# A hybrid decoder layer on one core: in-projection, shift and RWKV preparation as one program, the sample recurrence on VectorE, two places for the scores of short prompt rows

## The reference, cut to what matters

```python
h = rmsnorm(x); proj = h @ w_in                      # 1056 x 3328, 26 tiles of 128 rows
q, k, v, pr = split(proj)                            # 12 tiles attention, 14 tiles RWKV
m = pr + (shifted - pr) * mu                         # token shift: r, k, v, xw, xa, xg
w = exp(-exp(-softplus(-(w0 + tanh(xw) @ w2)) - .5)) # decay
a = sigmoid(a0 + xa @ a2); g = sigmoid(xg) @ g2
kk = k * k_k / norm(k * k_k);  k = k * (1 + (a - 1) * k_a)
# state, per head 64 x 64, over tokens:
s = s * w + (s @ -kk) (kk * a)^T + v k^T;  y = s @ r
bonus = sum(r * k * r_k) * v;  y = (groupnorm(y) + bonus) * g
# differential attention: softmax(q1 k1) - lam * softmax(q2 k2), causal for the prompt,
# over 1024 cached keys (8 pages) + 4 new ones for each sample group
x = x + rmsnorm(concat(attention, y) @ w_o)
# then a gated convolution FFN and a per-layer embedding, both with residuals
```

## Time and profile before

| what | value |
|---|---|
| median of 3 runs | 2543.29 us (2535.67 to 2544.15) |
| profiled execution, its own time | 2543.07 us |
| its span, first to last instruction | 2541.6 us |
| TensorE busy | 2033.1 us (80%) |
| VectorE busy | 1200.1 us (47%) |
| ScalarE busy | 855.9 us (34%) |
| GpSimd busy | 470.2 us (19%) |
| mean granted clock of TensorE | 0.874 |

### The profile page before, as it was taken

How to read it: one execution, slowest core, us unless ns; L and a number is a source line. 1 busy time by engine, 2 the same in 40 slices (tenths; PEclk the granted TensorE clock), 3 DMA queues, 4 the chain that set the end, 5 groups by cost and what they waited for, 6 DMA issues and landing times. The chain is left out here.

```text
span 2541.6 us, 39506 instructions
## 1 busy us (share of the span) xinstructions
PE 2033.1 (80%) x15324; PEld 1930.0 (76%) x15324; DVE 1200.1 (47%) x1772; ACT 855.9 (34%) x1422; POOL 470.2 (19%) x600
## 2 busy tenths in 40 slices
PE   1999963449999882546485669899999999999996
PEld 1999962338888881435254559899999999999996
DVE  5001016635555426996321135586543376653365
ACT  3111114313333322334201134554433355543342
POOL 0000002442313118990231200000000000000000
PEclk8999986769999955767766579999999999999998
DMA  2222222010000004103495024243234343233343
GB/s 99 92 84 101 84 102 99 37 32 1 0 0 0 0 16 98 37 13 84 156 332 160 35 79 147 75 150 129 89 103 131 110 157 121 92 97 117 94 131 123
DMA packets 83863, 229.34 MB, mean 90 GB/s; under 512 B 13394, under 2 KB 15186, under 8 KB 83442
## 3 DMA queue, kind: packets, MB, share of 16 engines
q1 hardware_dynamic: 72690, 191.25, 23.6%
q0 software_dynamic: 8864, 30.84, 3.3%
q10 hardware_dynamic: 2176, 5.42, 0.7%
HBM read 189.74 MB, written 37.73 MB: 89 GB/s over the span
## 5 line engine op out<-in xcount | busy, mean ns | idle before, releaser
L2403 PE MATMUL tl_acc<-tl_Hh,tl_wh 128*128 128x264 f32 x1536 | 438.9, 286 | 7.3 <-DVE tl_Hl L2681 7.3
L2403 PE MATMUL tl_acc<-tl_Hh,tl_wl 128*128 128x264 f32 x1536 | 437.1, 285 | 0.0
L2403 PE MATMUL tl_acc<-tl_Hl,tl_wh 128*128 128x264 f32 x1536 | 437.0, 284 | 0.0
L2723 DVE TENSOR_TENSOR tl_wl<-tl_raw,tl_wh 128x1024 fp32r<-128x1024 f32 (+2 forms) x184 | 208.3, 1132 | 422.9 <-ACT tl_wh L2552 422.7
L2552 ACT ACTIVATE tl_wh<-tl_raw 128x1024 fp32r<-128x1024 f32 (+2 forms) x184 | 181.0, 984 | 499.1 <-PE tl_acc L2403 450.9
L2403 PEld LDWEIGHTS tl_acc<-tl_Hh,tl_wh 128*128 128x128 f32 x1536 | 289.2, 188 | 8.5 <-DVE tl_Hl L2681 8.3
L2403 PEld LDWEIGHTS tl_acc<-tl_Hh,tl_wl 128*128 128x128 f32 x1536 | 290.0, 189 | 0.0
L2403 PEld LDWEIGHTS tl_acc<-tl_Hl,tl_wh 128*128 128x128 f32 x1536 | 289.4, 188 | 0.0
L690 PE MATMUL in_acc<-Hh,in_wh 128*128 128x352 f32 x624 | 202.6, 325 | 24.5 <-DVE in_wl L673 24.5
L690 PE MATMUL in_acc<-Hl,in_wh 128*128 128x352 f32 x624 | 201.1, 322 | 0.0
L690 PE MATMUL in_acc<-Hh,in_wl 128*128 128x352 f32 x624 | 201.0, 322 | 0.0
(11 more groups left out here) (359 smaller groups left out, 4446.9 us busy)
## 6 DMA issues: line engine op xcount, KB each, us to landing
tl_raw<-dram_w_up SPq DMA_DIRECT2D x88, 512.0 KB, 3.5
as_kT<-dram_k_pool SPq DMA_DIRECT2D x64, 256.0 KB, 5.0
as_vp<-dram_v_pool POOLq DMA_DIRECT2D x64, 256.0 KB, 4.9
tl_raw<-dram_w_down SPq DMA_DIRECT2D x32, 448.0 KB, 3.4
dram_projT<-in_out POOLq DMA_DIRECT2D x26, 528.0 KB, 3.0
in_raw<-dram_w_in SPq DMA_DIRECT2D x26, 512.0 KB, 3.5
ap_dup<-dram_projT SPq DMA_DIRECT2D x20, 512.0 KB, 8.1
tl_raw<-dram_w_pg SPq DMA_DIRECT2D x32, 320.0 KB, 3.2
```

What stands on the lines that cost most here:

```text
L2403: last = nc.tensor.matmul(out[:, n, 0:HP], w[:, u % 2, k, :], z, start=(begin and q == 0), stop=(end and q == 2))
L2723: tt(wl[:, u % 2, 0:kt], raw[:, u % 3, 0:kt], wh[:, u % 2, 0:kt].bitcast(F32), ALU.subtract).then_inc(S["residued"], 1)
```

## The change

Three parts.

**One program for stages 1 to 4.** A new function `front` takes the place of the constants' phases, `lam`, `rms_rows`, `scale_split`, `project` "in", `rwkv_mix`, `rwkv_prepare` and `SampleStates.dump`. The projection runs over half weight tiles (52 units `u`, 4 row blocks each), with three buffers for the raw weights. The columns are split into 512 (`accA`, two buffers) and two times 272 (`accB`, one buffer). `Hh`/`Hl` are made from x times gain without R, and VectorE multiplies by R when it evicts a tile (`evict`). The tiles come in another order: xw/xa and xg first, then v, k, r of each pair, then the 12 of attention. An evicted tile is mixed from SBUF without being read back. The preparation goes in 8 pieces (4 pairs, columns 0 to 511 and 512 to 1055), a piece in 5 steps, and each unit from 12 to 51 carries one step on each engine. NR, B and K, and V go to new HBM tensors (`nrS`, `bkS`, `vS`), and `rwkv_transitions` loads them: first the 128 columns of its first turn, then the rest.

**The sample recurrence** moves from GpSimd in `attend_prompt` to VectorE in `attend_sample`. It is cut into 16 parts, two a group; a sum over 64 is one `tensor_reduce` and no tree of additions. VectorE's loop over groups is written out in a new order.

**Scores.** In `attend_prompt` the units 1 and 3 of a head put their scores at column 512, and the units 1 to 3 wait for the exponential of two units before.

The diff, cut to its core (`rwkv_mix`, `rwkv_prepare` and `SampleStates.dump` are deleted as printed above; the preparation's steps on each engine hold the same operations as before over half the columns; `part_a` is 12 matmuls of 512 columns a unit, `part_b` 24 of 272; `PIECE_AT[q]` is 12 + 5q; `take` and `put` are a product and a sum over 128x2048, `read` a product and a `tensor_reduce`):

```diff
@@ attend_prompt @@
+        bank = lambda i: 512 if i in (1, 3) else 0
...
-        @block.gpsimd
-        def _(pool):
-            beside(pool, beside_done)
...
-                    if not early(j, u, 1):
+                    if not early(j, u, 1) and (i == 0 or i > 3):
                         pe.wait_ge(S["exped"], s * 2 - 1 + c)
+                    elif not early(j, u, 2):
+                        pe.wait_ge(S["exped"], s * 2 - 3 + c)
@@ attend_sample, VectorE @@
+            for n in range(NB):
+                fill(n, n % 2, n < 2)
+                beside(dve, 2 * n, S)
+                leave(n)
+                if n + 2 < NB:
+                    front(n + 2, n % 2, False)
+                beside(dve, 2 * n + 1, S)
@@ SampleStates @@
+    def decay(self, dve, t, S):
...
+        self.nc.vector.tensor_tensor(tmp[:], st[:], along_v(1), ALU.mult).then_inc(S["against_kk"], 1)
+        dve.wait_ge(S["against_kk"], t + 1)
+        self.nc.vector.tensor_reduce(sav[:], tmp[:], AX, ALU.add).then_inc(S["sa_summed"], 1)
+        self.nc.vector.tensor_tensor(st[:], st[:], along_v(0), ALU.mult).then_inc(S["decayed"], 1)
...
+    def recur(self, dve, part, S):
+
+        (self.decay, self.take, self.put, self.read)[part % 4](dve, part // 4, S)
@@ rwkv_transitions, SyncE and GpSimd @@
+            now, later = slice(0, 2 * C), slice(2 * C, SEQ)
+            for dst, src in ((BK, "bkS"), (V, "vS"), (NR, "nrS")):
+                sp.dma_start(dst[..., now], o[src][..., now]).then_inc(first_in, 16)
             for dst, src in consts:
                 sp.dma_start(dst[:], a[src]).then_inc(S["const_in"], 16)
+            for dst, src in ((BK, "bkS"), (V, "vS"), (NR, "nrS")):
+                sp.dma_start(dst[..., later], o[src][..., later]).then_inc(rest_in, 16)
...
+            pool.wait_ge(first_in, 48)
             place(0, 0, True)
...
+            pool.wait_ge(rest_in, 48)
             with pool.Fori(1, NCH // 2) as i:
@@ front, TensorE @@
+            def part_b(u, t, kh):
+                if kh == 0 and t:
+                    pe.wait_ge(S["evicted_b"], t)
...
+            for u in range(FU):
+                t, kh = u // 2, u % 2
+                if u == 2:
+                    spread_x()
+                for piece in piece_steps(u):
+                    prep(*piece)
+                pe.wait_ge(S["residued"], u + 1)
+                if kh == 0:
+                    part_a(u, t, kh)
+                    part_b(u, t, kh)
+                else:
+                    part_b(u, t, kh)
+                    part_a(u, t, kh)
+                if u == 1:
+                    totals()
@@ front, ScalarE @@
+            for u in range(FU + 1):
+                round_up(u + 1)
...
+                if u % 2 == 0 and 0 <= t < N_SHIFTED:
...
+                    nc.scalar.activation(dst_of(j), cur[:, t % 3], ACT.Copy, scale=omu[:, j:j + 1])\
...
+                for piece in piece_steps(u):
+                    prep(*piece)
@@ front, VectorE @@
+            for k in range(KD):
+                dve.wait_ge(S["high"], k + 1)
+                stt(Hl[:, k], X[:, k], param("g_mix_pre", KD)[:, k:k + 1], Hh[:, k].bitcast(F32), ALU.mult,
+                    ALU.subtract).then_inc(S["low"], 1)
...
+                    tt(acc[:], acc[:], sq[:, k % 2], ALU.add).then_inc(S["summed"], 1)
+            for u in range(FU + 1):
+                residue(u + 1)
...
+                t = u // 2 - 1
+                if u % 2 == 0 and 0 <= t < MT_IN:
+                    evict(t)
+                if u % 2 == 1 and 0 <= t < N_SHIFTED:
+                    mix(t)
...
+                for piece in piece_steps(u):
+                    prep(*piece)
```

More of the change, by code:

```diff
@@ L1154, in front, with fill @@
                                         ALU.mult).then_inc(S["combined"], 1)
-            def back(n, b, first):
+            def fill(n, b, first):
                 dve.wait_ge(S["turned"], n + 1)
@@ L1465, in rwkv_transitions @@
     S = {n: kit.sem("rt_" + n) for n in names}
+    first_in, rest_in = kit.sem("rt_first_in"), kit.sem("rt_rest_in")
     with ExitStack() as ctx:
@@ new lines, in read @@
+    def read(self, dve, t, S):
+        vec, st, tmp, ys = self.vec, self.st, self.tmp, self.ys
+        dve.wait_ge(S["added_v"], t + 1)
+        self.nc.vector.tensor_tensor(tmp[:], st[:], vec[:, t, 4, :].unsqueeze(1).broadcast_to([P, 32, 64]),
+                                     ALU.mult).then_inc(S["against_r"], 1)
+        dve.wait_ge(S["against_r"], t + 1)
+        self.nc.vector.tensor_reduce(ys[:, t, :], tmp[:], AX, ALU.add).then_inc(S["y_summed"], 1)
+    def recur(self, dve, part, S):
+        (self.decay, self.take, self.put, self.read)[part % 4](dve, part // 4, S)
+        if part == 4 * NT - 1:
+            dve.wait_ge(S["y_summed"], NT)
@@ L2829, in build @@
-        x_view = a["xT"].rearrange("(k p) t -> p k t", p=P)
-        proj = o["projT"].rearrange("(m p) t -> m p t", p=P)
-        with ExitStack() as ctx:
-            Hh = kit.sb(ctx, "Hh", [P, KD, T], F32R)
-            Hl = kit.sb(ctx, "Hl", [P, KD, T], F32R)
-            raw = weight_buffer(kit, ctx, "in", KD)
-            with ExitStack() as inner:
-                X = kit.sb(inner, "X", [P, KD, T])
-                R = kit.sb(inner, "R", [P, T])
-                rms_rows(kit, "rms_x", X, R[:], KD, ones[:], epsc[:, 0:1], ident[:],
-                         loads=[x_view[:, k] for k in range(KD)])
-                scale_split(kit, "split_x", X, KD, T, Hh, Hl, gain("g_mix_pre"), lambda k: R[:],
-                            ahead=first_units(raw, a["w_in"]))
-            parts = [(n * T3, T3) for n in range(3)]
-            project(kit, "in", MT_IN, KD, 1, a["w_in"], Hh, Hl, parts,
-                    lambda c: ToDram(kit, c, "in", parts, lambda m: proj[m] if isinstance(m, int) else
-                                     proj[ds(m, 1)].rearrange("a p t -> (a p) t")), raw)
+        ELC = kit.sb(top, "ELC", [P, NPAIR, NCH])
@@ L2850, in build @@
+        front(kit, a, o, par, param, ones[:], epsc, ident[:], identb[:], causal[:], blockcol[:], lam, ELC)
+        proj = o["projT"].rearrange("(m p) t -> m p t", p=P)
         kit.retire()
```

826 lines of the change are left out of this document (486 added, 340 removed).

## The result

| | before | changed |
|---|---|---|
| median | 2543.72 us (4 runs, 2535.67 to 2545.21) | **2346.97 us** (4 runs, 2343.28 to 2349.22) |
| ratio, with 95% interval | | **0.9231** (0.9208 to 0.9254): faster |
| profiled execution: own time, span | 2543.07, 2541.6 us | 2346.25, 2344.6 us |
| mean granted clock | 0.874 | 0.907 |

The prediction said 2354, with 2325 to 2425 as the range. SyncE's queue marks the borders of the stages. This is its timeline in the changed kernel (start, length, line, transfer): the first load of the transitions, the first of the sample attention, and the first transfer behind it. Between them stand the store of the prompt state, at 792.61, and the first load of the prompt attention, at 809.00.

A forecast was written before the change was run, and what follows sets the result against it. TensorE was taken to bound projection and tail, an engine-to-engine chain the preparation. Savings of 158.7 (front) and 72.2 (prompt), less 4 (transitions) and 37.6 (sample), make 189.3 off 2543.07: 2354 us, range 2325 to 2425.

The forecast's parts named there:

- likeliest case: Whole kernel: the forecast itself, 2354 us, given a chance of 76%.
- Front, start: Before TensorE's full stream: x arrives earlier, VectorE passes over 8 row blocks; full stream from 28.5 us, 32 us earlier.
- Front, stream: Projection on TensorE: 51 units 289.7 us, ramp 3, row sums and spreading 5.7, small products 45, waits 3.
- the cover: Front: read-back, mix and preparation work on VectorE, ScalarE and GpSimd lie under TensorE's stream, costed at nothing.
- the first rival: Front: the preparation does not stay hidden, TensorE waits out the chain; 71 us come back, 2425 us; chance 12%.
- Front, end: After the last product: eviction 0.8 us, turning 4.18, copy 3.35, then 4.38 to the next stage, reached at 387.6.
- the transitions: Transitions stage: new loads ahead of the constants delay the first placing; 4 us lost, 0 to 20.
- Prompt attention: Prompt attention without GpSimd's recurrence: earlier first peak, heads of 34 and 48.4 us; 72.2 us saved, 62 to 78.
- The scores' places: Prompt attention: the two places of the scores were costed at nothing, TensorE being held and ScalarE waiting for the load.
- Sample attention: Sample attention with the recurrence on VectorE: 119 us from the first fill, 84 before; 37.6 us lost, 32 to 44.
- TensorE's clock in the front: Front: waits at each unit could drop TensorE to its lower clock; all at 1.2 GHz gives 2694 us; chance 3%.
- V pages were not held up: Sample attention: VectorE's recurrence passes could delay GpSimd's page issues, some 55 us more, 2409 us; chance 8%.

## Why the prediction was right

Its total is 7 us above the measured time and its likeliest case is the one that came. By its own steps:

**Front, start** (28.5 predicted, 30.4 measured). The issue, arrival and rounding of x took longer (VectorE's first `Hl` stands at 10.8, not 7), the pairs of passes were shorter (2.40, not 2.6), and the second unit waited for the queued residue as described, for 5.6 us. Errors of 3.8 us for the first and -1.9 for all passes make the 1.9.

**Front, stream** (346.4 predicted from the first full unit to the last product, 348.6 measured). The bare tile was 11.58 and not 11.36, 5.6 us over the 51 units; the small products came to 42 by the stores, 45 predicted. The granted clock was 0.83 from 30 to 60 us and 1.00 from 60 to 372, so 30 x 0.17, some 5 us, went to the ramp where 3 had been taken. The waits that I put at 3 us (0 to 15) do not appear: behind the start of the second unit TensorE waits for another engine only twice, 1.0 us each, for the row factor and, when the stream is over, for the last eviction. That 5.6 and 2 too little and 3 and 3 too much nearly cancel is luck. The work under the stream was as counted, 165 us of VectorE where the prediction had 166. So the cover held, and taking it away cost 92 us, more than the 71 that the first rival had for it. That price was too low because it took off TensorE's 59.4 us at the clock of 0.70, where the same products cost 42 to 45 in the stream, and because the chain of half pieces is 137 us long and not 130.

**Front, end** (12.7 predicted, 11.9 measured) and **the transitions** (4 and 3.3): right in size and in the sum for the latter. The prediction adds the loads of the first columns and of the constants to 10 us, and the first placing came at 10.1; with the order turned round it came at 10.5. The rest of the columns came sooner than predicted (34.3 us, not 43), and TensorE did not wait for it.

**Prompt attention** (72.2 and 72.8): the first peak, the heads of 34 and 48 us and ScalarE's wait in them came as written. Taking GpSimd's work back cost the 72 us again, and moving the load took the wait out of the heads. So this term is right in its mechanism and not only in its sum.

**The scores' places** (nothing, and nothing): right, though half of the reason given for it fell.

**Sample attention** (37.6 lost predicted, 30.0 measured): the term that missed most. It was 7.6 us too high, and the smaller errors of the other terms, the front's 3.3 us among them, cancel. A pass takes 2.27 to 2.29 us (2.3), the groups 15.2 to 15.6 and 14.5 to 15.2 (15.7 and 14.8), and the raw sum of 113.7 was 112.0. But I had added 5.3 us for TensorE at half its clock, which would have made the scores 2 us later still. The odd groups wait 1.55 to 2.30 us for scores, and the prediction's 6.7 - 0.4 - 4.6 = 1.7 already held that. TensorE's timelines show it: the 16 products of the scores behind the peak at 1287.04 and of the next group, before, and those of the last odd group in the changed kernel.

```profile
1284.89 1.92 PE L1107 MATMUL as_sc<-as_kT,as_qb 128*32 128x512 f32 x16
1296.15 3.64 PE L1107 MATMUL as_sc<-as_kT,as_qb 128*32 128x512 f32 x16 [1.60 <-issue]
```
```profile
1134.37 2.55 PE L1106 MATMUL as_sc<-as_kT,as_qb 128*32 128x512 f32 x16
```

The three odd groups have 1.92, 2.26 and 2.55 us. So the window's clock of 0.66 costs these scores 0.6 us at most, and not 2.

**The rivals.** The preparation stayed hidden. TensorE's clock in the front was 0.99. V pages were not held up: GpSimd issued them 1.23 us apart with the recurrence beside it and 1.22 to 1.23 before. Two issues of the kernel before:

```profile
1286.30 0.54 POOL L1015 DMA_DIRECT2D as_vp<-dram_v_pool  x1 [18.11 <-issue]
1287.53 0.54 POOL L1015 DMA_DIRECT2D as_vp<-dram_v_pool  x1 [0.69 <-issue]
```

The Trainium skill, in "SBUF — State Buffer", section "Who interferes with whom", has it that products of two SBUF tensors (by inference) and reduces do not stop the writing of descriptors; the traces agree, for 128x2048 passes of 2.28 us.

## What to carry to other kernels

A chain from engine to engine, laid under a stream of one busy engine, is worth its length in the open less what it adds to the stream, and the way to price it is to take the cover away: 92 us here. Work moved to an idle engine costs by where it stands in the queue: the same 82 us of VectorE made the sample stage 36 us longer (151.4 against 115.4) in a loop that then waits for them, and 12 when a part of them stood in VectorE's own waits for loads, two of the sixteen parts in the stage ahead. Read what waits behind what in the DMA queue as well: a load behind a store of other data was worth 28 us, more than many a change of the arithmetic.

## What the hardware showed that was not expected

GpSimd's copies of 128x128 were slowed up to eightfold (0.30 to 2.45 us) beside VectorE's 128x2048 products, while its DMA issues kept their 1.23 us. In the prompt attention it went the other way too: VectorE's 276 instructions took 221 us beside GpSimd's products and 128 without them, though each engine works on tiles of its own. Not every instruction was slowed. These are groups of VectorE in the prompt attention (count, busy time, mean ns), three before and the same three after: the subtraction of two SBUF tensors, the peak of scores in PSUM, and the product of a weight tile in SBUF with a factor for each row.

```profile
L880 DVE TENSOR_TENSOR ap_kl<-ap_dup,ap_kh 128x1024 fp32r<-128x1024 f32 x10 | 29.7, 2974 | 0.0
L887 DVE TENSOR_REDUCE ap_small<-ap_sc 128x1 f32<-128x1024 f32 x8 | 9.7, 1214 | 0.0
L902 DVE TENSOR_SCALAR ap_wgt<-ap_pexp,ap_small 128x128 f32<-128x128 f32 x4 | 8.8, 2212 | 0.0
```
```profile
L878 DVE TENSOR_TENSOR ap_kl<-ap_dup,ap_kh 128x1024 fp32r<-128x1024 f32 x10 | 12.1, 1219 | 0.0
L885 DVE TENSOR_REDUCE ap_small<-ap_sc 128x1 f32<-128x1024 f32 x8 | 9.7, 1216 | 0.0
L900 DVE TENSOR_SCALAR ap_wgt<-ap_pexp,ap_small 128x128 f32<-128x128 f32 x4 | 1.1, 276 | 0.0
```

The peaks took the same to 2 ns, the subtractions 2.4 times as long beside GpSimd, and the products with a factor up to eight times. The Trainium skill, in "SBUF — State Buffer", section "Who interferes with whom", has a rule that bears on both: a VectorE instruction with two SBUF inputs and a GpSimd instruction that reads SBUF shut each other out for a whole instruction; by it such a copy would take at most 0.30 + 2.28 = 2.58 us, an estimate from these rows, and 2.45 was the longest. The products with a factor have only one SBUF tensor besides the factor, so it stays open whether this rule covers them.

The same state took GpSimd 4.5 us for a product of 128x2048 while VectorE stood still (4.49), and VectorE 2.28, and VectorE's `tensor_reduce` over 2048 elements (2.29) took no longer than a product, where GpSimd's tree of additions needed 5.3 to 8.1.
